# A head's norm behind the second projection instead of the first, and the finest level tiles in one bank of PSUM

## The chip, the core and the metric

The kernel runs on one core of a Trainium2 chip. The metric is the device time of one execution in microseconds (us), as the median of several runs. TensorE does the matrix products, VectorE (DVE) and ScalarE (ACT) read PSUM and work on SBUF, GpSimd (POOL) works on SBUF alone, and the queue of SyncE (SP) starts most transfers. Each engine executes its instructions strictly in the order in which they are written and waits on semaphores.

## What is computed

The reference is one layer of a decoder trunk for a prompt of 1024 tokens and 8 sample sequences. One input projection feeds three parallel token mixers: a gated linear recurrence with 4 heads of 128 keys by 128 values (branch A), a second recurrence behind a convolution (B) and a sparse attention (C). The merged result goes through an output projection and a layer norm. The change touches branch A alone:

```
qa = silu(aq); log_f = logaddexp(log(lb), log1p(-lb) + log_sigmoid(af)); ka = -expm1(log_f)
oa, s_new = hgrn2_chunked(qa, ka, ai, log_f, s0)        # prompt; hgrn2_recurrent for the samples
ya = (group_rms(oa).reshape(B, T, A_WIDTH) * a_norm_g) * silu(az)
```

`group_rms` divides each head's output by the root of its mean square over the 128 values: this is the norm that moves.

## The kernel before

All engines walk through one written plan, `a_items(h)` for h = 0 to 4. In pass h the projections of head h are computed (items P0, P1, ...; in pass 4 gate projections G0, G1, ... take their place) and between them stand the chunks of the recurrence of head h-1 (items R0 to R7, one for each 128 tokens), and the norm of head h-2 (item N). Each engine runs its own part of an item, in the plan's order.

- A projection item is 24 products of 128 by 344 columns (`split_product`, L1023): 8 blocks of the inner dimension, three products each of a high and a low part. P0 to P2 fill two banks in turn (ring `pq`), the others use banks 3 and 4 (ring `pf`). ScalarE takes a tanh or a copy of the result (L1993, L1999), VectorE multiplies (L2550).
- R c is, on TensorE, `a_levels`: the products of chunk c's attention matrix, 7 levels from 64 x 64 down to 32 x 32 blocks (L1566 to L1579), then a transpose (L1586) for the key, and then `a_output` of the chunk before (L1599 to L1602). Levels of 8 down to 1 (i = 3 to 6) each have a tile of 128 columns: three in bank 5, the last in bank 6. On VectorE R c is `a_att`: it waits for the level products, and five COPY_PREDICATED (L2594) gather their tiles under masks. The fifth signals `att_masked`, for which the next chunk's `a_levels` waits, since it writes the same tiles.
- N is, on TensorE, `a_norm`: three products of the squares with a matrix of ones (L1617 into bank 2 behind the key's transpose, and two by L1620 into the ring `pf`). They wait for `sq_ready`, ScalarE's square (L2059) of the head's output at the end of the pass before (item Q). ScalarE then takes Ln of the three results (L2070) and Exp of the whole (L2072), each behind a load of its function table, and signals `rms_ready`. VectorE multiplies the output by gain and gate (L2614) and, after `rms_ready`, by the norm (L2616).

Item N stands in passes 2, 3 and 4 right behind the first projection (heads 0, 1 and 2; below the first, second and third norm). Head 3's norm is the last item of all. The first R0's transpose in a pass waits for `rms_ready`, because the norm's product lies in its bank (L1585).

Of the kernel before, what the change touches and what calls it, by code (L numbers as in the profile page):

```python
# [27 lines left out]
P = 128  # L28
# [5 lines left out]
TC = NS + T  # L34
CH = TC // 3
# [237 lines left out]
def layer_program(nc, ctx, a, o):  # L273
# [13 lines left out]
    ps = ctx.enter_context(nc.psum_tensor("ps", [P, 8, 512], F32))  # L287
# [234 lines left out]
    def e(name):  # L522

        if name not in ev:
            ev[name] = sem(name)
        return ev[name]  # L540
# [38 lines left out]
    def a_items(h):  # L579


        if h == 4:
            plan = "G0 N G1 R0 G2 R1 G3 R2 G4 R3 G5 R4 G6 S R5 G7 R6 G8 O R7 G9 Z Q G10 G11 N"
        elif h % 2:
            plan = "P0 N P1 R0 P2 R1 P3 P4 R2 P5 R3 P6 P7 R4 P8 S R5 P9 R6 P10 O R7 P11 Z F Q"
        else:
            plan = "P0 N P1 R0 P2 R1 P3 P4 R2 P5 R3 P6 R4 P7 S R5 P8 R6 P9 O R7 P10 Z F Q"
        items, norm = [], h - 2
        for x in plan.split():
            if x == "N":  # L590
                if norm >= 0:
                    items.append((x, norm))
                norm += 1
            elif x[0] in "PGF" or h:
                items.append((x[0], int(x[1:] or 0)))
        return items

    def a_product(h, i):

# [412 lines left out]
    def _(pe):  # L1012
        mm = nc.tensor.matmul
# [542 lines left out]
        def a_levels(h, c):  # L1556
            S = AS[h % 2]
            q = 4 * h + c // 2
            pe.wait_ge(e("x_ready"), q + 1)
            pe.wait_ge(e("att_masked"), natt[0] + 1)  # L1560
            natt[0] += 1
            cc = slice(P * (c % 2), P * (c % 2) + P)
            tc = slice(NS + P * c, NS + P * c + P)
            for g in range(4):
                gp, c0 = slice(32 * g, 32 * g + 32), 32 * g
                mm(ps[gp, 5, c0:c0 + 32], lhsT=XQ[:, q % 2, 9, cc.start + c0:cc.start + c0 + 32],  # L1566
                   rhs=S["q"][:, tc.start + c0:tc.start + c0 + 32], start=True, stop=True)
            for i in range(3):
                m = LEVELS[i]
                for s0 in range(0, P, 2 * m):  # L1570
                    c0 = P * (c % 2) + s0
                    mm(ps[s0:s0 + m, 5, s0 + m:s0 + 2 * m], lhsT=XQ[:, q % 2, i, c0:c0 + m], rhs=XQ[:, q % 2, i, c0 + m:c0 + 2 * m],  # L1572
                       start=True, stop=True)
            for i in range(3, 7):
                bank, p0 = (5, P * (i - 2)) if i < 6 else (6, 0)
                for g in range(4):
                    c0 = 32 * g
                    x = XQ[:, q % 2, i, cc.start + c0:cc.start + c0 + 32]
                    last = mm(ps[c0:c0 + 32, bank, p0 + c0:p0 + c0 + 32], lhsT=x, rhs=x, start=True, stop=True)  # L1579
            last.then_inc(e("att_full"), 1)  # L1580
            i = 8 * h + c
            if i >= 1:
                pe.wait_ge(e("kot_ready"), i)
            if c == 0 and h:
                pe.wait_ge(e("rms_ready"), h)  # L1585
            nc.tensor.transpose(ps[:, 2, 0:P], XQ[:, q % 2, 8, cc], ID).then_inc(e("kot_full"), 1)  # L1586

        def a_output(h, c):
# [23 lines left out]
        def a_norm(h):  # L1612
            sq = AS[h % 2]["bk"]
            pe.wait_ge(e("sq_ready"), h + 1)
            if h < 3:
                pe.wait_ge(e("kot_ready"), 8 * h + 8)
                mm(ps[:, 2, P:P + CH], lhsT=ONES, rhs=sq[:, 2 * CH:TC], start=True, stop=True)  # L1617
            for c in range(2 if h < 3 else 3):
                b = pf.acquire(pe)
                mm(ps[:, 3 + b, 0:CH], lhsT=ONES, rhs=sq[:, CH * c:CH * c + CH], start=True, stop=True).then_inc(pf.full, 1)  # L1620
# [122 lines left out]
    def _(act):  # L1743
# [317 lines left out]
        def a_norm(h):  # L2061

            sq = AS[h % 2]["bk"]
            for c in range(3):
                if c < 2 or h == 3:
                    b = pf.take(act)
                    src, free = ps[:, 3 + b, 0:CH], pf.free
                else:
                    src, free = ps[:, 2, P:P + CH], None
                st(A(sq[:, CH * c:CH * c + CH], src, ACT.Ln, bias=G[:, GEPS:GEPS + 1], scale=0.25 / P), free)  # L2070

            st(A(sq, sq, ACT.Exp, scale=-0.5), e("rms_ready"))  # L2072
# [98 lines left out]
    def _(v):  # L2171
# [412 lines left out]
        def a_att(h, c):  # L2584
            natt[0] += 1
            i = 8 * h + c
            if i == 0:
                st(V.memset(ATT, 0.0))
            v.wait_ge(e("att_full"), natt[0])
            if i >= 2:  # L2590
                v.wait_ge(e("chunk_full"), i - 1)
            for l in range(5):
                tile = ps[:, 5, P * l:P * l + P] if l < 4 else ps[:, 6, 0:P]
                st(V.copy_predicated(ATT[:, i % 2], LM[:, 2 + l].bitcast(U16), tile), e("att_masked") if l == 4 else None)  # L2594
            st.mark(e("att_ready"))

# [226 lines left out]
```

## Time and profile before

| | us |
|---|---|
| median of 3 runs | 1654.55 |
| lowest and highest | 1649.14, 1655.98 |
| the profiled execution's own time | 1653.34 |
| its span in the profile | 1651.3 |
| TensorE busy | 1528.5 (93%) |
| TensorE loading weights | 1372.2 (83%) |
| VectorE, ScalarE, GpSimd busy | 828.8, 563.8, 569.1 |
| TensorE's share of the chain that ended last | 53% (42% of the span is L1023) |

The page's busy shares say which engine fills the span; the chain that ended last says what the end waited for at each moment. A row of a timeline gives an operation's start, its busy time and, in brackets, how long the engine had been idle before it and what released it.

### The profile page before, as it was taken

Reading aid. Unit: us, or ns where it says so; the run is one execution under the profiler, and the core shown is the slowest. Engines: PE = TensorE matmul, PEld = TensorE weight load, DVE = VectorE, ACT = ScalarE, POOL = GpSimd, SP = SyncE. Lnnn points to the kernel's source line nnn. Section 1 sums busy time; section 2 is a strip of 40 time slices with the busy share of each in tenths; the row PEclk is TensorE's granted clock in tenths of the full one; section 3 lists DMA queues with packets and bytes.
Section 4 is the critical chain, followed back from the end, with each engine's and each line's share of the span. In section 5 each row is a group of like instructions: output and inputs, shape, how many; then the busy total and the mean of one; then the engine's idle time right before and its main releaser. Section 6 shows DMA issues by size and latency. Waiting matters only on the chain.

```text
span 1651.3 us, 35632 instructions
## 1 busy us (share of the span) xinstructions
PE 1528.5 (93%) x14484; PEld 1372.2 (83%) x14484; DVE 828.8 (50%) x1555; ACT 563.8 (34%) x1128; POOL 569.1 (34%) x833
## 2 busy tenths in 40 slices
PE   5899889999998999999989999999899988999997
PEld 4899866666667888888879998889798887999997
DVE  3640557666661233333324256757552655456588
ACT  1213135545451333333312353745432765001100
POOL 2233000000004111221032577888772252346700
PEclk8999989999998999999999999999899999999999
DMA  9510120000006344434251411203032121544422
GB/s 332 176 51 28 28 91 2 1 1 1 1 20 177 90 117 132 121 117 120 70 182 41 129 27 39 81 27 105 31 102 74 29 60 33 200 154 144 165 91 78
DMA packets 136852, 143.20 MB, mean 87 GB/s; under 512 B 17110, under 2 KB 126706, under 8 KB 135922
## 3 DMA queue, kind: packets, MB, share of 16 engines
q1 hardware_dynamic: 127362, 127.03, 25.0%
q10 hardware_dynamic: 9328, 13.90, 2.3%
q8 instruction: 115, 1.88, 0.5%
q14 instruction: 47, 0.39, 0.1%
HBM read 115.62 MB, written 29.40 MB: 88 GB/s over the span
## 4 chain that ended last, share of the span: by engine, by line
PE 53%; POOL 6%; ACT 4%; DVE 3%; issue 2%; DMA 0%; SPq 0%; ACTq 0%; DVEq 0%; POOLq 0%; PEldq 0%
PE ps L1023 42%; PE ps L1385 2%; PE ps L1372 2%; POOL w_lo L907 1%; ACT xq L2042 1%; POOL vs_spread L977 1%; POOL dd L957 1%; PE ps L1034 1%; POOL dd L958 1%; POOL sts L974 1%; PE ps L1609 1%; POOL w_hi L903 1%; POOL sts L979 1%; PE ps L1572 1%; PE ps L1668 1%
## 5 line engine op out<-in xcount | busy, mean ns | idle before, releaser
L1023 PE MATMUL ps<-w_hi,h_hi 128*128 128x256 f32 x704 | 203.7, 289 | 5.9 <-DVEq L152 2.9
L1023 PE MATMUL ps<-h_hi,w_hi 128*128 128x344 f32 x600 | 199.9, 333 | 9.2 <-POOL w_lo L907 6.1
L1023 PE MATMUL ps<-w_lo,h_hi 128*128 128x256 f32 x704 | 198.9, 283 | 1.1 <-issue 1.1
L1023 PE MATMUL ps<-w_hi,h_lo 128*128 128x256 f32 x704 | 198.8, 282 | 0.0
L1023 PE MATMUL ps<-h_lo,w_hi 128*128 128x344 f32 x600 | 194.1, 324 | 0.0
L1023 PE MATMUL ps<-h_hi,w_lo 128*128 128x344 f32 x600 | 193.6, 323 | 0.0
L903 POOL CAST w_hi<-w_raw 128x512 fp32r<-128x512 f32 (+1 forms) x96 | 64.9, 676 | 280.1 <-DMA w_raw<-in_w_in 107.0
L907 POOL TENSOR_TENSOR w_lo<-w_raw,w_hi 128x256 fp32r<-128x256 f32 (+1 forms) x192 | 151.0, 817 | 3.9
L1023 PE MATMUL ps<-h_hi,wg_hi 128*128 128x344 f32 x432 | 143.8, 333 | 1.4 <-DVE pcs L2420 0.8
L1023 PEld LDWEIGHTS ps<-w_hi,h_hi 128*128 128x128 f32 x704 | 134.2, 191 | 10.0 <-DVEq L152 3.3
L1023 PE MATMUL ps<-h_lo,wg_hi 128*128 128x344 f32 x432 | 138.9, 322 | 0.0
L1023 PE MATMUL ps<-h_hi,wg_lo 128*128 128x344 f32 x432 | 138.8, 321 | 0.0
L1023 PEld LDWEIGHTS ps<-w_lo,h_hi 128*128 128x128 f32 x704 | 134.1, 190 | 0.0
L1023 PEld LDWEIGHTS ps<-w_hi,h_lo 128*128 128x128 f32 x704 | 134.0, 190 | 0.0
L920 POOL TENSOR_TENSOR qt<-qt,to 128x512 f32<-128x512 f32 x16 | 20.3, 1267 | 314.7 <-DVE to L2390 314.7
L1023 PEld LDWEIGHTS ps<-h_hi,w_hi 128*128 128x128 f32 x600 | 115.5, 193 | 12.4 <-POOL w_lo L907 6.8
L1023 PEld LDWEIGHTS ps<-h_lo,w_hi 128*128 128x128 f32 x600 | 115.0, 192 | 0.7 <-issue 0.2
L1023 PEld LDWEIGHTS ps<-h_hi,w_lo 128*128 128x128 f32 x600 | 115.0, 192 | 0.0
L1862 ACT ACTIVATE pr<-ps,nm 128x640 f32<-128x640 f32 (+7 forms) x128 | 88.4, 697 | 39.0 <-DVE nm L2350 32.7
L930 POOL CAST wg_hi<-w_raw 128x512 fp32r<-128x512 f32 x36 | 22.1, 614 | 220.9 <-PE ps L1023 177.9
L1023 PEld LDWEIGHTS ps<-h_hi,wg_hi 128*128 128x128 f32 x432 | 82.1, 190 | 12.3 <-issue 8.3
L1281 PE MATMUL ps<-const_g,pr 128*128 128x128 f32 x560 | 82.0, 279 | 10.2 <-DVE pt L2358 3.5
(463 smaller groups left out, 3568.3 us busy)
## 6 DMA issues: line engine op xcount, KB each, us to landing
w_raw<-in_w_in SPq DMA_DIRECT2D x46, 512.0 KB, 4.4
sgm<-gate_spill SPq DMA_DIRECT2D x22, 516.0 KB, 6.2
gate_spill<-gate_stage ACTq DMA_DIRECT2D x54, 172.0 KB, 2.4
w_raw<-in_w_in SPq DMA_DIRECT2D x34, 256.0 KB, 4.6
adw<-in_ada_w SPq DMA_DIRECT2D x8, 1024.0 KB, 11.6
pgc<-in_cache_nsa_kv SPq DMA_DIRECT2D x64, 128.0 KB, 2.8
pg<-in_cache_nsa_kv SPq DMA_DIRECT2D x64, 128.0 KB
w_raw<-in_w_branch SPq DMA_DIRECT2D x12, 512.0 KB, 5.0
```

The lines of the kernel that those rows point to most:

```text
L903: last = nc.gpsimd.tensor_copy(hi[:, kj, 0:width], raw[:, j:j + 2])
L907: last = nc.gpsimd.tensor_tensor(lo[:, kj, 0:width], raw[:, j:j + 1], hi[:, kj, 0:width].bitcast(F32), SUB)
L920: st(nc.gpsimd.tensor_tensor(d3, d3, TO[:, i % 2, :].rearrange("p (a c) -> p a c", a=4), ADD), e("to_added"))
L930: st(nc.gpsimd.tensor_copy(hi[:, j:j + 4], raw[:, j:j + 4]))
L957: st(nc.gpsimd.tensor_tensor(dv[:, :, 0, :], ref, kv_[:, :, 0, :], SUB))
L958: st.fire(nc.gpsimd.tensor_tensor(dv[:, :, 1, :], bv[:, :, 1, :], ref, SUB), e("d_ready"))
L974: st(nc.gpsimd.tensor_tensor(STS[:, b:b + 2], STS[:, b:b + 2], decay[:, b:b + 2].unsqueeze(2).to_broadcast([P, 2, P]), MUL))
L1023: last = mm(out, lhsT=l, rhs=r, start=(first and i == 0 and j == 0), stop=(final and i == n - 1 and j == 2), skip_group_check=joint)
L1281: last = nc.tensor.transpose(ps[:, 4 + way, P * i:P * i + P], PR[:, u % 2, P * j:P * j + P], ID)
L1372: last = mm(ps[half, bank + q, P * j:P * j + P], lhsT=buf[:, s, j, 256 * par + c:256 * par + c + 64], rhs=ID, start=True, stop=True)
L1385: last = mm(ps[:, 3, P * c:P * c + P], lhsT=W1S[:, c, j].rearrange("p x o -> p (x o)"), rhs=CMT[:, c, :, j, :], start=(j == 0), stop=(j == 7))
L1862: st.fire(A(PR[:, u % 2, P * n * g:P * n * g + P * n], src, ACT.Exp, bias=NM[:, 4 * (u % 2) + g:4 * (u % 2) + g + 1], scale=-1.0, accum_ou ...
```

## The change

The norm item N moves behind the second projection in every plan (`P0 P1 N R0` for `P0 N P1 R0`). The four finest level tiles now begin 32 columns apart in bank 5, so that they overlap in columns but not in the 32 x 32 blocks that are used. Bank 6 is thereby free and takes the norm's first product. With it go two waits of TensorE: the norm's for the last key of the head before (`kot_ready`) and the transpose's for `rms_ready`. One is added: the norm's first product waits for the `rms_ready` of the norm before.

```diff
--- before.py
+++ after.py
@@ -580,11 +580,11 @@
 
 
         if h == 4:
-            plan = "G0 N G1 R0 G2 R1 G3 R2 G4 R3 G5 R4 G6 S R5 G7 R6 G8 O R7 G9 Z Q G10 G11 N"
+            plan = "G0 G1 N R0 G2 R1 G3 R2 G4 R3 G5 R4 G6 S R5 G7 R6 G8 O R7 G9 Z Q G10 G11 N"
         elif h % 2:
-            plan = "P0 N P1 R0 P2 R1 P3 P4 R2 P5 R3 P6 P7 R4 P8 S R5 P9 R6 P10 O R7 P11 Z F Q"
+            plan = "P0 P1 N R0 P2 R1 P3 P4 R2 P5 R3 P6 P7 R4 P8 S R5 P9 R6 P10 O R7 P11 Z F Q"
         else:
-            plan = "P0 N P1 R0 P2 R1 P3 P4 R2 P5 R3 P6 R4 P7 S R5 P8 R6 P9 O R7 P10 Z F Q"
+            plan = "P0 P1 N R0 P2 R1 P3 P4 R2 P5 R3 P6 R4 P7 S R5 P8 R6 P9 O R7 P10 Z F Q"
         items, norm = [], h - 2
         for x in plan.split():
             if x == "N":
@@ -594,6 +594,10 @@
             elif x[0] in "PGF" or h:
                 items.append((x[0], int(x[1:] or 0)))
         return items
+
+    def level_tile(l):
+
+        return P + 32 * (l - 1) if l else 0
 
     def a_product(h, i):
 
@@ -1572,17 +1576,15 @@
                     mm(ps[s0:s0 + m, 5, s0 + m:s0 + 2 * m], lhsT=XQ[:, q % 2, i, c0:c0 + m], rhs=XQ[:, q % 2, i, c0 + m:c0 + 2 * m],
                        start=True, stop=True)
             for i in range(3, 7):
-                bank, p0 = (5, P * (i - 2)) if i < 6 else (6, 0)
+                p0 = level_tile(i - 2)
                 for g in range(4):
                     c0 = 32 * g
                     x = XQ[:, q % 2, i, cc.start + c0:cc.start + c0 + 32]
-                    last = mm(ps[c0:c0 + 32, bank, p0 + c0:p0 + c0 + 32], lhsT=x, rhs=x, start=True, stop=True)
+                    last = mm(ps[c0:c0 + 32, 5, p0 + c0:p0 + c0 + 32], lhsT=x, rhs=x, start=True, stop=True)
             last.then_inc(e("att_full"), 1)
             i = 8 * h + c
             if i >= 1:
                 pe.wait_ge(e("kot_ready"), i)
-            if c == 0 and h:
-                pe.wait_ge(e("rms_ready"), h)
             nc.tensor.transpose(ps[:, 2, 0:P], XQ[:, q % 2, 8, cc], ID).then_inc(e("kot_full"), 1)
 
         def a_output(h, c):
@@ -1613,8 +1615,9 @@
             sq = AS[h % 2]["bk"]
             pe.wait_ge(e("sq_ready"), h + 1)
             if h < 3:
-                pe.wait_ge(e("kot_ready"), 8 * h + 8)
-                mm(ps[:, 2, P:P + CH], lhsT=ONES, rhs=sq[:, 2 * CH:TC], start=True, stop=True)
+                if h:
+                    pe.wait_ge(e("rms_ready"), h)
+                mm(ps[:, 6, 0:CH], lhsT=ONES, rhs=sq[:, 2 * CH:TC], start=True, stop=True)
             for c in range(2 if h < 3 else 3):
                 b = pf.acquire(pe)
                 mm(ps[:, 3 + b, 0:CH], lhsT=ONES, rhs=sq[:, CH * c:CH * c + CH], start=True, stop=True).then_inc(pf.full, 1)
@@ -2066,7 +2069,7 @@
                     b = pf.take(act)
                     src, free = ps[:, 3 + b, 0:CH], pf.free
                 else:
-                    src, free = ps[:, 2, P:P + CH], None
+                    src, free = ps[:, 6, 0:CH], None
                 st(A(sq[:, CH * c:CH * c + CH], src, ACT.Ln, bias=G[:, GEPS:GEPS + 1], scale=0.25 / P), free)
 
             st(A(sq, sq, ACT.Exp, scale=-0.5), e("rms_ready"))
@@ -2590,7 +2593,7 @@
             if i >= 2:
                 v.wait_ge(e("chunk_full"), i - 1)
             for l in range(5):
-                tile = ps[:, 5, P * l:P * l + P] if l < 4 else ps[:, 6, 0:P]
+                tile = ps[:, 5, level_tile(l):level_tile(l) + P]
                 st(V.copy_predicated(ATT[:, i % 2], LM[:, 2 + l].bitcast(U16), tile), e("att_masked") if l == 4 else None)
             st.mark(e("att_ready"))
```

On TensorE, pass 2 around the first norm, before (`ak` holds the squares, `aq` and `xq` the recurrence's factors; the names behind "waits" are semaphores):

```order
L1023 MATMUL ps<-h_hi,w_lo 128x344
L1617 MATMUL ps<-ak_168,ones 128x344 [waits kot_ready,sq_ready]
L1620 MATMUL ps<-ak_168,ones 128x344 [waits pf_free] x2
L1023 MATMUL ps<-h_hi,w_hi 128x344 [waits pq_free]
...
L1566 MATMUL ps<-aq_171,xq 32x32 [waits x_ready,att_masked,pf_free,pq_free]
...
L1586 MATMUL ps<-const_g,xq 128x128 [waits rms_ready,kot_ready]
L1023 MATMUL ps<-h_hi,w_hi 128x344 [waits pq_free]
...
L1566 MATMUL ps<-aq_171,xq 32x32 [waits att_masked,x_ready]
```

And with the change:

```order
L1027 MATMUL ps<-h_hi,w_lo 128x344
L1620 MATMUL ps<-ak_168,ones 128x344 [waits sq_ready]
L1623 MATMUL ps<-ak_168,ones 128x344 [waits pf_free] x2
L1570 MATMUL ps<-aq_171,xq 32x32 [waits x_ready,att_masked,pf_free,pq_free]
...
L1588 MATMUL ps<-const_g,xq 128x128 [waits kot_ready]
L1027 MATMUL ps<-h_hi,w_hi 128x344 [waits pq_free]
...
L1570 MATMUL ps<-aq_171,xq 32x32 [waits att_masked,x_ready]
```

The 24 products of P1, which stood between the norm and the levels of R0, now stand ahead of the norm; P2, between the levels of R0 and those of R1, stays where it was.

On VectorE at the same place, before (`sga` is ScalarE's tanh, `ot` the head's output, `att` the attention matrix, `lm` the masks):

```order
L2571 TENSOR_TENSOR xq<-xq,aq_171 128x256 [waits eb_ready,own_dve]
L2550 SCALAR_TENSOR_TENSOR aq_167<-sga,ps 128x344 [waits own_dve,d_exp,sg_ready]
L2614 SCALAR_TENSOR_TENSOR ot<-ot,prm,az_170 128x1032 [waits sq_ready,pq_free]
L2616 TENSOR_TENSOR ot<-ot,ak_168 128x1032 [waits rms_ready,own_dve]
L2550 SCALAR_TENSOR_TENSOR aq_167<-sga,ps 128x344 [waits sg_ready,ya_done]
L2594 COPY_PREDICATED att<-lm,ps 128x128 [waits chunk_full,att_full,pq_free]
L2594 COPY_PREDICATED att<-lm,ps 128x128 [waits own_dve] x4
```

And with the change:

```order
L2574 TENSOR_TENSOR xq<-xq,aq_171 128x256 [waits eb_ready,own_dve]
L2553 SCALAR_TENSOR_TENSOR aq_167<-sga,ps 128x344 [waits own_dve,d_exp,sg_ready]
L2553 SCALAR_TENSOR_TENSOR aq_167<-sga,ps 128x344 [waits sg_ready,pq_free]
L2617 SCALAR_TENSOR_TENSOR ot<-ot,prm,az_170 128x1032 [waits sq_ready,pq_free]
L2619 TENSOR_TENSOR ot<-ot,ak_168 128x1032 [waits rms_ready,own_dve]
L2597 COPY_PREDICATED att<-lm,ps 128x128 [waits chunk_full,att_full,ya_done]
L2597 COPY_PREDICATED att<-lm,ps 128x128 [waits own_dve] x4
```

P1's multiplication has moved ahead of the norm's two operations; the masks of R0 stand directly behind them.

## Rows read from the trace of the kernel before

**Rows 1.** The page: the span, and TensorE's granted clock in 40 slices, in tenths.
```profile
span 1651.3 us, 35632 instructions
...
PEclk8999989999998999999999999999899999999999
```

**Rows 2.** Timeline of TensorE, first norm: start, us busy, operation, idle before and releaser.
```profile
1032.62 0.32 PE L1023 MATMUL ps<-h_hi,w_lo 128*128 128x344 f32 x1
...
1034.38 0.85 PE L1617 MATMUL ps<-ak,ones 128*128 128x344 f32 x2 [1.44 <-ACT ak L2059]
...
1035.96 0.58 PE L1023 MATMUL ps<-h_hi,w_hi 128*128 128x344 f32 x1
...
1040.08 0.27 PE L1566 MATMUL ps<-aq,xq 128*32 128x32 f32 x8
...
1041.41 0.30 PE L1586 MATMUL ps<-const_g,xq 128*128 128x128 f32 x1 [0.27 <-ACT ak L2072]
...
1045.40 0.27 PE L1566 MATMUL ps<-aq,xq 128*32 128x32 f32 x8
```

**Rows 3.** The chain that ended last, 1020 to 1060 us: one projection group of 24 products.
```profile
1041.71 3.77 PE ps L1023 x24
```

**Rows 4.** Timeline of ScalarE, first norm.
```profile
1035.88 1.28 ACT L2070 ACT_TABLE_LOAD   x1 [1.07 <-PE ps L1620]
...
1038.90 1.28 ACT L2072 ACT_TABLE_LOAD   x1
...
1040.20 1.06 ACT L2072 ACTIVATE ak<-ak 128x1032 f32<-128x1032 f32 x1
```

**Rows 5.** Timeline of VectorE, first norm.
```profile
1041.36 1.32 DVE L2616 TENSOR_TENSOR ot<-ot,ak 128x1032 f32<-128x1032 f32 x1 [3.22 <-ACT ak L2072]
...
1043.26 1.67 DVE L2594 COPY_PREDICATED att<-lm,ps 128x128 f32<-128x128 uint16 x5
```

**Rows 6.** Timeline of TensorE, second and third norm.
```profile
1105.70 0.56 PE L1617 MATMUL ps<-ak,ones 128*128 128x344 f32 x1 [1.79 <-ACT ak L2059]
...
1116.72 0.27 PE L1566 MATMUL ps<-aq,xq 128*32 128x32 f32 x8
...
1180.79 0.84 PE L1617 MATMUL ps<-ak,ones 128*128 128x344 f32 x2 [1.44 <-ACT ak L2059]
...
1184.19 0.43 PE L1023 MATMUL ps<-h_hi,w_hi 128*128 128x344 f32 x1 [1.40 <-ACT ak L2070]
...
1193.19 0.27 PE L1566 MATMUL ps<-aq,xq 128*32 128x32 f32 x8
```

**Rows 7.** Timeline of VectorE, second and third norm.
```profile
1112.69 1.33 DVE L2616 TENSOR_TENSOR ot<-ot,ak 128x1032 f32<-128x1032 f32 x1 [4.07 <-ACT ak L2072]
...
1187.78 1.45 DVE L2616 TENSOR_TENSOR ot<-ot,ak 128x1032 f32<-128x1032 f32 x1 [3.86 <-ACT ak L2072]
```

**Rows 8.** Waits of GpSimd, 1116 to 1163 us: for whom, total, times, longest.
```profile
POOL dd L957 <- ACT xq L2042: 2.9, 2, 2.3
POOL w_hi L903 <- PEq L1540: 0.8, 1, 0.8
```

**Rows 9.** Timeline of TensorE: three longer waits elsewhere.
```profile
1017.39 2.56 PE L1609 MATMUL ps<-aq,sts 128*128 128x1 f32 x16 [1.95 <-POOL sts L979]
...
1162.51 3.57 PE L1609 MATMUL ps<-aq,sts 128*128 128x1 f32 x16 [2.65 <-POOL sts L979]
...
1331.50 0.65 PE L1023 MATMUL ps<-h_hi,w_hi 128*128 128x344 f32 x1 [4.41 <-POOL w_lo L907]
```

**Rows 10.** Windows of 1 us: length, PE busy (instructions), granted clock, DMA, GB/s.
```profile
1161.00:1162.00 1.00, 0.00 (x0) 0.95 0.00 0
1162.00:1163.00 1.00, 0.49 (x3) 0.50 0.00 0
...
1172.00:1173.00 1.00, 1.00 (x8) 0.93 0.00 0
...
1335.00:1336.00 1.00, 1.00 (x6) 0.51 0.00 0
```

## The prediction

> **What bounds the kernel now.** I read the page first: TensorE is busy nearly throughout, at its full clock (2.4 GHz) in most slices and below it in a few [rows 1]. Then I listed TensorE's waits in the stretch of branch A, and read the timelines of the engines at each moved norm. TensorE bounds this stretch, so a microsecond in which it has nothing to do counts, unless a later wait gives it back.
>
> At the first norm the last product of P0 starts at 1032.62; the norm's first product comes at 1034.38 after 1.44 us idle, for ScalarE's square. So P0 ends at 1032.94. P1 follows the norm at 1035.96, the levels of R0 come at 1040.08, the transpose at 1041.41 after 0.27 us idle for the norm's Exp, P2 then, and the levels of R1 at 1045.40 [rows 2]. P2 takes 3.77 us [rows 3]. The norm itself occupies TensorE for 1.58 us (1034.38 to 1035.96).
>
> ScalarE is slower at the norm: a table load of 1.28 us from 1035.88, three Ln, a second load, and an Exp that ends at 1040.20 + 1.06 = 1041.26 [rows 4]. VectorE, which had been idle for 3.22 us for this, multiplies from 1041.36 for 1.32 us and masks R0's tiles from 1043.26 for 1.67 us, to 1044.93 [rows 5]. The levels of R1 wait for these masks. Before the change they are ready 0.47 us ahead of TensorE. That margin is what the reader should keep in view.
>
> At the second norm TensorE idles 1.79 us, at the third 1.44 and then 1.40 us, since G1 needs a bank of ring `pf` that the norm's second product holds until ScalarE has read it [rows 6].
>
> **The change part by part.** Removed: the idle time ahead of the norms, 1.44 + 1.79 + 1.44 us; the third norm's 1.40 us for a bank; and 0.27 us twice at the transpose (seen at the first norm; the second's is taken as the same). Together 6.6 us. P1 fills the time instead, and the square is ready when it ends.
>
> Added: P1 no longer stands between the norm and the masks of R0. Call T0 the start of the norm's products. From T0 to VectorE's multiplication is 6.98 us (1034.38 to 1041.36) [rows 2, 5], and 6.99 us at both others (1105.70 to 1112.69, 1180.79 to 1187.78) [rows 6, 7]. This chain goes through the products, two table loads and the Exp, and nothing of it gets shorter. Behind it VectorE has 1.32, 1.33 or 1.45 us of multiplication and 1.67 us of masks, with some 0.03 us between, and some 0.1 us until TensorE is released (my estimate, after the 0.10 us from the Exp's end at 1041.26 to 1041.36). So R1 can start at T0 + 10.1, 10.1 and 10.2 us. TensorE itself gets there sooner: norm 1.58, levels 1.33 - 0.27 = 1.06, transpose about 0.3, P2 3.77, in all T0 + 6.7 us. A new wait of 3.4 us ahead of R1's levels takes the place of the old ones.
>
> T0 in the new order is the end of P0 plus one projection group:
>
> - first norm: 1032.94 + 3.77 = 1036.71; R1 at 1046.8 where it was 1045.40 [rows 2, 3, 5]: 1.4 us later.
> - second: 1105.70 - 1.79 + 3.77 = 1107.68; R1 at 1117.8 where it was 1116.72 [rows 6, 7]: 1.1 us later.
> - third: 1180.79 - 1.44 + 3.77 = 1183.12; R1 at 1193.35 where it was 1193.19 [rows 6, 7]: 0.2 us later. G2 needs the bank as G1 did, 3.40 us behind the norm's start (1180.79 to 1184.19); by then 2.9 us of other work have passed, so the wait splits into some 0.4 and 3.1 us.
>
> The sum of these is 2.7 us longer.
>
> Then the clock. In the windows, TensorE idle from 1159.86 to 1162.51 lost its full clock near 1161.95; the granted clock was 0.50 (1.2 GHz) until about 1172 [rows 9, 10]. I went through all of TensorE's waits of 1.3 us and more behind the start-up: six are of 2.65 to 4.41 us (the shortest and longest are shown), and at each the clock fell; three are of about 2 us (1.95 is shown), and at two of them it fell; none of the shorter ones, the norms' 1.44 and 1.79 us among them, made it fall [rows 2, 6, 9]. The change has three waits of 3.1 to 3.4 us where it had 1.4 to 1.8 us. A fall costs half of the low time in which TensorE works: 1162.51 to 1172.07 is 9.6 us, so 4.8 us; behind the wait that ended at 1331.50 the clock was back near 1335.9, so 2.2 us [rows 9, 10]. Behind R1's levels dense projections follow at once, so I take 3.0 us, between the bounds: 9.0 us for three falls, with 6.6 and 14.4 us as bounds, and 0 if none falls.
>
> The Trainium skill, "TensorE: Matmul & The Clock Gate", section "Why this matters for your kernels", advises to leave no long idle gaps between bursts of products, because the engine then goes back to half rate. By that rule the sum is the one with falls; without it, it is the 2.7 us alone. The trace agrees with it at all six waits of 2.65 us and more.
>
> What costs nothing: the overlapping tiles take the same 16 products per chunk and the same five mask reads, so neither TensorE nor VectorE has more to do. The added wait on the previous `rms_ready` is over by tens of microseconds (1041.26 against 1105.70). ScalarE's two table loads stay two. Its key copy and the nine Exp of the next pair of chunks start some 2 us later, and with them GpSimd's last differences; what needs them is R2, two projection groups (7.5 us) behind R1, so they stay hidden by some microsecond. If that cover were gone, R2 would be late by another 1 us.
>
> Does a later wait give the delay back? TensorE waits 2.65 us for GpSimd's sample states at 1162.51 [rows 9]. But GpSimd had waited 0.8 us for TensorE to release weights, and had 2.9 us of waits for ScalarE's Exp, in the 1116 to 1163 us that lead there [rows 8]; the former is at 1131.9, and behind it GpSimd works with hardly a gap. So GpSimd starts that work later by as much as TensorE is late, and the wait stays.
>
> Sum: 1653.34 + 2.7 + 9.0 = 1665.0 us against the profiled execution. The median of the runs is 1654.55, 1.2 us above it, within their spread of 1649.14 to 1655.98; I give 1665.
>
> **The rivals.** What a measurement of this kernel can tell from no change is about 0.5%, 8.3 us.
>
> - The new waits come, but the clock mostly holds (none or one fall). For it speaks that a fall at a 2 us wait is not certain; against it, that six of six longer ones fell. It gives +2.7 to +5.7 us, 1657 to 1660. Chance 0.18.
> - Not slower, the gain stays: this happens if the masks of R0 end before TensorE is through with P2. Then 6.6 us are saved, 1648 us. It needs the norm's chain of 6.98 us plus 3.0 us on VectorE to shrink to under 6.7 us; break-even is where it shrinks by 0.9 us at each norm. Nothing in the change shortens it, except that weights of ones may load ahead while P1 still runs (0.2 us at most). With a fall of the clock saved near 1162 as well (4.8 us) it would be past 0.5%. Chance 0.06.
> - The change does nothing: the delay is taken back in the waits of 1.95 to 2.65 us for the sample states, as far as GpSimd isn't held up by TensorE, and falls of the clock only change places. 1654 us. Chance 0.08.
>
> **How the numbers follow.** My forecast, new waits with two or three falls, has 0.68: 1653.34 + 2.7 + 2 x 2.2 = 1660.4 at least and + 2.7 + 14.4 = 1670.4 at most. The range of 1656 to 1671 takes in nearly all of the first rival as well, and leaves out the other two. Slower by over 0.5% (above 1662.8): nearly all of the forecast's 0.68, less the 0.04 in which two falls are cheap, plus 0.01 from a first rival with a dear fall: 0.65. Faster by over 0.5%: half of the second rival, 0.03. Within 0.5%: 0.32.
>
> **What would show it.** Right: TensorE's norm products directly behind P1, with no idle time; a wait of 3.1 to 3.4 us ahead of the levels of R1 (L1570) in passes 2, 3 and 4, released by VectorE; a granted clock of 0.50 behind at least two of them; TensorE's idle time at the norm gone. VectorE's masks of R0 directly behind its norm multiplication. Wrong would be: masks of R0 ready before P2 ends; a clock at 1.00 through all three waits; or a wait for the sample states that has shrunk by what the norms lost.

## The result: slower by a third of a per cent

Measured together, the changed kernel takes 1656.66 us (median, 1652.62 to 1662.35) and the kernel before 1652.36 us: a ratio of 1.0033 with a 95% interval of 1.0024 to 1.0043 (the quotient of the two medians alone is 1.0026). Two more measurements of the unedited change gave 1.0049 and 1.0038 (runs 5 and 10 below). By the means, each against the kernel before measured beside it, the change is 5.0, 8.8 and 7.1 us slower, with standard errors of 0.8 to 1.0 us. All its 30 executions have a mean of 1658.3 us, and 72 of the kernel before, those of runs 1 to 12, have one of 1653.0 us. That is 5.3 us (standard error 0.6), but it mixes chips in unequal parts. The forecast was 10.4 us above the median shown and 11.7 us above the profiled execution. The direction and the waits came as forecast; the price of the clock did not.

The page of the changed kernel, its profiled execution (1658.82 us):

```profile
span 1656.9 us, 35628 instructions
...
PEclk7999999999998999999999999999999999999999
```

The span is 5.6 us longer than before's [rows 1]. The tenths of the granted clock look no worse, so falls can't be counted there: each lasts under 11 us, a quarter of a slice of 41 us.

TensorE's timeline at the three norms, the rows that answer to [rows 2, 6]:

```profile
1036.17 0.74 PE L1620 MATMUL ps<-ak,ones 128*128 128x344 f32 x2
...
1037.99 0.27 PE L1570 MATMUL ps<-aq,xq 128*32 128x32 f32 x8
...
1042.76 0.32 PE L1027 MATMUL ps<-h_hi,w_lo 128*128 128x344 f32 x1
1046.11 0.34 PE L1570 MATMUL ps<-aq,xq 128*32 128x32 f32 x8 [3.04 <-DVE att L2597]
...
1057.91 0.27 PE L1570 MATMUL ps<-aq,xq 128*32 128x32 f32 x8
...
1110.82 0.74 PE L1620 MATMUL ps<-ak,ones 128*128 128x344 f32 x2
...
1120.77 0.34 PE L1570 MATMUL ps<-aq,xq 128*32 128x32 f32 x8 [3.05 <-DVE att L2597]
...
1131.23 0.27 PE L1570 MATMUL ps<-aq,xq 128*32 128x32 f32 x8
...
1186.93 0.74 PE L1620 MATMUL ps<-ak,ones 128*128 128x344 f32 x2
...
1196.87 0.27 PE L1570 MATMUL ps<-aq,xq 128*32 128x32 f32 x8 [2.61 <-DVE att L2597]
...
1203.53 0.27 PE L1570 MATMUL ps<-aq,xq 128*32 128x32 f32 x8 [1.12 <-DVEq L152]
```

What matters in them is that the norm's products (L1620) have no idle time ahead of them any more, and that the levels of R1 (the second L1570 of a norm) now wait 3.04, 3.05 and 2.61 us for VectorE's masks. The last row is the third norm's R2, which waits as well. VectorE there, against [rows 5]:

```profile
1037.54 1.29 DVE L2617 SCALAR_TENSOR_TENSOR ot<-ot,prm,az 128x1032 f32<-128x1032 f32 x1
1043.06 1.23 DVE L2619 TENSOR_TENSOR ot<-ot,ak 128x1032 f32<-128x1032 f32 x1 [4.23 <-ACT ak L2075]
1044.33 1.64 DVE L2597 COPY_PREDICATED att<-lm,ps 128x128 f32<-128x128 uint16 x5
```

The level products of R0 had ended by 1039.1, but their masks start at 1044.33, behind a multiplication for which VectorE idles 4.23 us. From the norm's first product to R1 it is 1046.11 - 1036.17 = 9.94 us; the forecast was 10.1.

Windows around R1 of the first norm (four rows), of the second (three) and of the third (the columns are length, then busy us and instructions of PE, PEld, DVE, ACT, POOL, then the granted clock, DMA share and GB/s):

```profile
1044.00:1045.00 1.00, 0.00 (x0) 0.00 (x0) 0.90 (x3) 0.94 (x3) 0.92 (x2) 1.00 0.00 0
1045.00:1046.00 1.00, 0.00 (x0) 0.00 (x0) 0.90 (x3) 0.91 (x4) 1.00 (x3) 0.68 0.92 326
1050.00:1051.00 1.00, 1.00 (x6) 1.00 (x5) 0.90 (x4) 0.00 (x0) 1.00 (x2) 0.50 0.01 2
1053.00:1054.00 1.00, 1.00 (x8) 1.00 (x7) 0.92 (x2) 0.00 (x0) 0.92 (x3) 1.00 1.13 342
1120.00:1121.00 1.00, 0.23 (x8) 0.23 (x8) 0.82 (x3) 0.94 (x3) 1.00 (x3) 0.72 0.98 343
1123.00:1124.00 1.00, 1.00 (x6) 1.00 (x6) 0.96 (x2) 0.40 (x2) 1.00 (x3) 0.57 0.41 115
1124.00:1125.00 1.00, 1.00 (x9) 1.00 (x8) 0.90 (x4) 0.00 (x0) 1.00 (x2) 1.00 0.00 0
1197.00:1203.00 6.00, 5.41 (x83) 4.97 (x78) 5.34 (x15) 3.75 (x10) 5.61 (x13) 1.00 0.57 171
```

The clock fell at the first two waits, for 6.8 and 3.4 us, and held at the third (1.00 from 1197 to 1203). In the profiles of both kernels each stretch of low clock between 1000 and 1260 us lasted 3.4, 6.8 or 10.2 us.

**Where the time went.** One measure serves for all kernels here: the start of a chunk's levels, counted from the end of ScalarE's square (before 1034.32, 1105.64 and 1180.73; after 1033.96, 1108.95 and 1184.72). Up to the square nothing at the norm differs.

| us behind the square's end | norm 1: R1, R2 | norm 2: R1, R2 | norm 3: R1, R2 |
|---|---|---|---|
| before | 11.08, 20.33 | 11.08, 20.33 | 12.46, 17.93 |
| after | 12.15, 23.95 | 11.82, 22.28 | 12.15, 18.81 |
| later | 1.07, 3.62 | 0.74, 1.95 | -0.31, 0.88 |

R1's delay is the late start. What R2 has beyond it at the first two norms is the low clock: 2.5 and 1.2 us. At the third norm the clock held, R1 was 0.3 us early, and R2 0.9 us late by its own wait. From the last levels of pass 1 (before 1020.68) to those of pass 4 (1229.99) the stretch is 5.1 us longer. It is less than the sum of the row, 3.62 + 1.95 + 0.88, because the low clock behind the wait for the sample states, 10.2 us long before [rows 10], was 6.8 us long after. Another execution of the kernel before (run 9) also has 6.8 us there, so this is no work of the change. In the profiles of runs 5 and 10 the stretch is 8.0 and 7.8 us longer than before's.

### The profile page after: what moved, and what is told of

Read it like the earlier page. It is cut to its first block, busy times and chain, and to the rows that moved or that the text cites. A ratio compares the mean times of both kernels' runs of the same rounds, so it can differ in the third digit from the quotient of the medians.

```text
span 1656.9 us, 35628 instructions
## 1 busy us (share of the span) xinstructions
PE 1531.5 (92%) x14484; PEld 1374.8 (83%) x14484; DVE 828.1 (50%) x1555; ACT 564.3 (34%) x1128; POOL 571.3 (34%) x833
## 4 chain that ended last, share of the span: by engine, by line
PE 55%; POOL 6%; DVE 4%; ACT 3%; issue 2%; DMA 0%; SPq 0%; ACTq 0%; DVEq 0%; POOLq 0%; PEldq 0%
PE ps L1027 43%; PE ps L1389 2%; PE ps L1376 2%; POOL w_lo L911 1%; POOL vs_spread L981 1%; POOL dd L961 1%; PE ps L1038 1%; POOL dd L962 1%; POOL w_hi L907 1%; POOL sts L978 1%; PE ps L1611 1%; PE ps L1671 1%; POOL sts L983 1%; PE ps L1576 0%; DVE att L2597 0%
## 5 line engine op out<-in xcount | busy, mean ns | idle before, releaser
L1027 PEld LDWEIGHTS ps<-h_hi,w_hi 128*128 128x128 f32 x600 | 115.8, 193 | 10.2 <-POOL w_lo L911 6.5
L1865 ACT ACTIVATE pr<-ps,nm 128x640 f32<-128x640 f32 (+7 forms) x128 | 88.5, 697 | 38.0 <-DVE nm L2353 31.6
```

Of the source, the lines that this page charges most:

```text
L1027: last = mm(out, lhsT=l, rhs=r, start=(first and i == 0 and j == 0), stop=(final and i == n - 1 and j == 2), skip_group_check=joint)
L1865: st.fire(A(PR[:, u % 2, P * n * g:P * n * g + P * n], src, ACT.Exp, bias=NM[:, 4 * (u % 2) + g:4 * (u % 2) + g + 1], scale=-1.0, accum_ou ...
```

## The experiments

The twelve runs in the order in which they ran. Each ratio is against the kernel before on the same chip, with its 95% interval; runs 5 to 8 ran on one chip, the others on another.

| run | median us (executions) | ratio |
|---|---|---|
| 1 products in the wait | 1658.37 (8) | 1.0028 (1.0016 to 1.0040) |
| 2 masks ahead of the norm on VectorE | 1650.37 (8) | 0.9977 (0.9967 to 0.9988) |
| 3 tiles and bank alone | 1650.80 (12) | 0.9984 (0.9975 to 0.9992) |
| 4 order alone | 1663.68 (5) | 1.0064 (1.0051 to 1.0077) |
| 5 the change again | 1659.93 (5) | 1.0049 (1.0035 to 1.0063) |
| 6 products in all four waits | 1657.57 (5) | 1.0036 (1.0022 to 1.0050) |
| 7 no table loads | 1651.45 (11) | 0.9997 (0.9988 to 1.0006) |
| 8 masks and tanh first | 1657.88 (5) | 1.0045 (1.0030 to 1.0059) |
| 9 the kernel before again | 1654.21 (12) | 1.0000 (0.9989 to 1.0011) |
| 10 the change, third time | 1660.08 (6) | 1.0038 (1.0024 to 1.0052) |
| 11 third norm alone | 1655.21 (12) | 1.0006 (0.9995 to 1.0017) |
| 12 masks first at two norms | 1649.40 (6) | 0.9970 (0.9958 to 0.9982) |

The theory was that the wait ahead of R1 is paid twice, by late starts and by the clock; the rivals were that the clock costs little, and that the tiles' new places cost something of their own.

### 1 and 6: is it the clock?

The idle time ahead of R1 is filled with products whose result nobody reads, into a free bank, so that TensorE keeps busy and R1 starts no sooner.

```diff
+        def keep_busy(h, n):
+            pe.wait_ge(pf.free, pf.p - 1)
+            b = (pf.p - pf.p0) % 2
+            w = wslot(U_A + 2 * h if h < 4 else U_G)
+            for k in range(n):
+                mm(ps[:, 3 + b, 0:CH], lhsT=w[0][:, k % 8, 0:P], rhs=H[0][:, k % 8, 0:CH], start=True, stop=True)
...
+                    if h >= 2 and i == 1:
+                        keep_busy(h, 16)
                     a_levels(h - 1, i)
```

Run 1:

> The changed kernel, with 16 products of 344 columns into a free bank behind P2 (G2), ahead of the levels of R1, in passes 2, 3 and 4: some 2.5 us of work without use, inside a wait that the changed kernel's profile shows as 3.04, 3.05 and 2.61 us. Theory one, two terms: the changed kernel lost 2.7 us by late starts of R1 and R2 and about 3 us by the clock that fell at these waits. Then this kernel keeps the 2.7 us and loses the rest: ratio to the kernel before 1.0010 to 1.0020, idle time ahead of R1 under 0.7 us, granted clock 1.00 there. Theory two, no clock term: the falls only change places, all 5.5 us are late starts. Then the ratio stays at 1.0033.

Run 6 has 17 such products in passes 2 and 3, 15 in pass 4, and 8 more ahead of pass 4's R2:

> As the first kernel with useless products, now 17 of them ahead of R1 in passes 2 and 3, 15 in pass 4, and 8 ahead of R2 in pass 4, where that kernel had a wait of 1.56 us and a fall. Idle time left ahead of R1 some 0.4 us. Theory one, a clock term on top of late starts: the late starts remain (R2 1.1 and 0.8 us later than before, counted from the end of the square, at the first two norms, R3 0.9 us at the third), no fall between the norm and R3: ratio 1.0012 to 1.0022, 0.001 to 0.002 below the changed kernel beside it. Theory two, no clock term on balance: the same ratio as the changed kernel beside it.

TensorE's timeline of run 6, R1 and R2 of the second norm, and a window over both:

```profile
1120.58 0.27 PE L1570 MATMUL ps<-aq,xq 128*32 128x32 f32 x8 [0.37 <-DVE att L2609]
...
1129.83 0.27 PE L1570 MATMUL ps<-aq,xq 128*32 128x32 f32 x8
```

```profile
1116.00:1126.00 10.00, 9.63 (x111) 9.23 (x110) 7.84 (x17) 6.79 (x16) 7.89 (x15) 1.00 0.42 130
```

The idle time was 0.25 to 0.37 us, no fall was left between the norms and R3, and R1 and R2 came 12.18 and 21.43 us behind the square's end at the first norm, 11.88 and 21.13 at the second, 12.17 and 18.91 at the third. Against before that is 1.1, 0.8 and 1.0 us later at R2: the late starts without the clock, 2.9 us in all. The clock's extra 2.5 and 1.2 us of the changed kernel are gone. So at the place the clock's share is shown. Run 1 is alike at R1 (idle time of 0.39 to 0.52 us, clock at 1.00), but kept a wait of 1.56 us ahead of pass 4's R2, with a fall behind it.

In the time of the whole kernel the share is hard to find, and both ratios lie above what a theory with a clock term expected. Run 6 is 2.7 us (mean) faster than run 5 on the same chip. Run 1, by its distance from the kernel before beside it, is 2.8 us faster than run 10 and 0.7 us faster than the first measurement; each of these three has a standard error of 1.0 to 1.3 us. Pooled, runs 1 and 6 have a mean of 1657.6 us in 13 executions, 0.8 us (standard error 0.7) below the change's 30.

An execution's mean granted clock gives its low time, the time at half clock: twice the span times the part of the full clock that is missing. Further below it serves to compare whole executions.

### 2: is it the order on VectorE?

```diff
                     a_att(h - 1, i)
+                    if i == 0 and h >= 2:
+                        a_norm(h - 2)
...
-                elif kind == "N":
+                elif kind == "N" and i == 3:
                     a_norm(i)
```

> The changed kernel, but on VectorE the norm's two operations of heads 0, 1 and 2 stand behind the masks of R0 and ahead of the factors. Theory one, the masks of R0 behind the norm's chain make R1 late: then the wait of 2.6 to 3.0 us ahead of R1 goes, the levels of R1 start some 6.8 us behind the norm's products instead of 9.94. R2 then waits up to 1.1 us for the factors, which come at the same time as before. Net 1 to 1.5 us per norm faster than the kernel before at the first two, about 0 at the third, and no falls there: ratio to before 0.996 to 0.999. Theory two, the wait has another cause (ScalarE's key copy, or the bank): the wait and the ratio of 1.0033 stay.

VectorE and TensorE at the first norm:

```profile
1038.31 1.66 DVE L2597 COPY_PREDICATED att<-lm,ps 128x128 f32<-128x128 uint16 x5 [1.66 <-PE ps L1583]
...
1042.20 1.23 DVE L2619 TENSOR_TENSOR ot<-ot,ak 128x1032 f32<-128x1032 f32 x1 [0.79 <-ACT ak L2075]
1043.47 2.96 DVE L2580 TENSOR_TENSOR xq<-xq,aq 128x128 f32<-128x128 f32 x5
```

```profile
1042.15 0.27 PE L1570 MATMUL ps<-aq,xq 128*32 128x32 f32 x8
1052.40 0.27 PE L1570 MATMUL ps<-aq,xq 128*32 128x32 f32 x8 [0.93 <-DVEq L152]
```

The masks start 5.2 us behind the square's end, where the changed kernel has them at 10.4, R1 waits for nothing, and the kernel is faster than both others. The wait did not vanish whole: VectorE's factors for chunks 2 and 3 (L2580) are late by the norm, and R2 waits 0.93, 0.94 and, in pass 4, 2.36 us for them. R2 still comes 1.0, 1.4 and 0.6 us earlier than before; a fall behind the last of these waits makes pass 4's R3 0.8 us late.

### 3 and 4: the two halves of the change

Run 3 has the changed kernel's tiles, bank and waits with before's three plans; run 4 has before's tiles, bank and waits with the new plans.

> One part of the change alone: the overlapping tiles and the norm's product in bank 6, with the norm behind the first projection as in the kernel before. Theory one, all of the loss comes from the moved norm: ratio 0.999 to 1.000, since only the 0.27 us twice at the transpose go. Rival, products or mask reads in one crowded bank are slower: five mask reads longer than 1.67 us or the level products longer, 32 chunks long, ratio 1.002 to 1.003.

> The other part alone: the norm behind the second projection, with the tiles, the norm's product and the two waits as in the kernel before. The transpose of R0 waits for the norm's Exp, which is ready 6.9 us behind the norm's start, when the levels end 2.7 us behind it. Theory one: a wait of some 4.2 us ahead of P2 (G2), R1 at the norm's start + 11.0 us, so 1 us per norm later than in the changed kernel, 5.7 us later than before in all, and falls of the clock at most of the waits, 3 to 8 us more: ratio 1.005 to 1.008. Theory without a clock term: 5.7 + 2.8 us for what the changed kernel shows beyond 2.7, whatever its cause, ratio 1.005.

Run 3, R0's transpose and R1 of the first norm, and run 4, R0's transpose, in TensorE's timeline:

```profile
1040.85 0.33 PE L1588 MATMUL ps<-const_g,xq 128*128 128x128 f32 x1
1044.87 0.27 PE L1570 MATMUL ps<-aq,xq 128*32 128x32 f32 x8
```

```profile
1041.95 0.45 PE L1586 MATMUL ps<-const_g,xq 128*128 128x128 f32 x1 [4.03 <-ACT ak L2072]
```

The freed bank takes the transpose's 0.27 us away at the first two norms; levels and masks last as long as before. That is a gain of 0.6 us by the timeline; the measured 0.16% (2.6 us) has an interval down to 1.3 us, and is more than was expected. Its low time is 85.7 us against 91.1 beside it, which fits the rest but doesn't show its cause. So the overlapping tiles cost nothing that these runs show, and what slows the change is the order. In before's bank the order costs more: the transpose waits 4.03 us for the Exp at all three norms, ahead of P2 instead of behind it, and R1 comes 15.78, 14.33 and 15.28 us behind the square's end, the low clock behind each of these waits included.

### 7: how much of it are the table loads?

ScalarE takes Abs in place of Ln for the norms of heads 0 to 2, which needs no other function table than the Exp. This kernel computes other values for these norms.

```diff
-ACT.Ln, bias=G[:, GEPS:GEPS + 1]
+ACT.Ln if h == 3 else ACT.Abs, bias=G[:, GEPS:GEPS + 1]
```

> The changed kernel, in which ScalarE takes an absolute value in place of the Ln for heads 0, 1 and 2, so that no function table is loaded at these norms (the norm's values are then not the reference's). The chain from the norm's products to the masks' end is 2.56 us shorter. Theory one, this chain sets R1: the wait ahead of R1 shrinks from 3.0 to some 0.5 us, R1 starts 9.6 us behind the square's end where it was 12.15 (11.08 before), R2 too comes earlier than before: ratio 0.997 to 0.999. Rival, VectorE's or GpSimd's other work sets R1: the wait stays above 2 us.

ScalarE's and TensorE's timelines, first norm:

```profile
1034.71 1.71 ACT L2073 ACTIVATE ak<-ps,const_g 128x344 f32<-128x344 f32 x3 [0.70 <-PE ps L1623]
1036.45 1.07 ACT L2075 ACTIVATE ak<-ak 128x1032 f32<-128x1032 f32 x1
```

```profile
1040.70 0.27 PE L1570 MATMUL ps<-aq,xq 128*32 128x32 f32 x8 [0.50 <-DVE att L2597]
```

Two loads of 1.28 us gone take 2.5 us off the wait at the first two norms (3.04 to 0.50, 3.05 to 0.57) and 1.9 us at the third (2.61 to 0.75). R1 comes 9.64, 9.34 and 9.89 us behind the square's end, earlier than before. So the loads are most of the wait. The ratio is 0.0036 to 0.0052 below the change's, but misses the expected 0.997 to 0.999: R2 comes 1.4, 1.7 and 0.7 us earlier than before, and the mean is lower by only 0.9 us (standard error 0.8). In pass 4 R2 waits 1.79 us with a fall behind it, and low time is 92.9 us against 85.1 beside it. What brought the other low time wasn't looked into.

### 8: a further step that failed

On top of run 2, ScalarE takes the tanh of the third projection group ahead of R0's Exp, and VectorE all factors of chunks 2 and 3 in R1.

```diff
+                    if i == 0 and h >= 2:
+                        a_group(h, 2) if h < 4 else a_gate(2)
...
+                    if h >= 2 and i < 2:
+                        if i:
+                            a_factors(h - 1, 1, range(8))
```

> The kernel with VectorE's norm behind the masks of R0, and in passes 2, 3 and 4 also: ScalarE's tanh of P2 (G2) ahead of the nine Exp of R0, and VectorE's factors of the second pair of chunks all in R1, behind its masks. In its parent R2 waited 0.93 us twice for these factors. Theory one: that wait goes, R2 starts 18.3 us behind the square's end where it was 20.33 before: 2.0 and 2.4 us saved at the first two norms, little at the third, where GpSimd's differences come late: ratio 0.996 to 0.998. If the masks of R1 or the factors are late in the new order: a new wait ahead of R2, ratio as its parent's 0.9977 or above.

TensorE's timeline, R2 of the first and the third norm:

```profile
1051.47 0.27 PE L1570 MATMUL ps<-aq,xq 128*32 128x32 f32 x8 [1.94 <-DVEq L152]
...
1201.40 0.33 PE L1570 MATMUL ps<-aq,xq 128*32 128x32 f32 x8 [6.17 <-DVEq L152]
```

VectorE's, first norm, R1:

```profile
1047.12 0.29 DVE L2609 COPY ot<-ps 128x128 f32<-128x128 f32 x1 [3.38 <-SPq L781]
```

R2 waits longer instead of less, 6.17 us in pass 4, where only one group lies between R1 and R2. VectorE's factors are what R2 needs. They were put off until R1, and there they stand behind two copies for which VectorE idles 3.38 us (4.25 us at the third norm). What the tanh alone does wasn't tried.

### 5, 9 and 10: the same kernels again

> The changed kernel once more, unedited, for a second look at which waits the clock falls at and for a time beside the next kernel on one chip. Both theories: ratio 1.0025 to 1.0040, the wait of some 3 us ahead of R1 three times. The theory of a clock term: a fall at two or three of these waits; the theory that falls only change places: one or two, and fewer falls than in the kernel before elsewhere between 1000 and 1250 us.

> The kernel before, unedited, to see what its own falls of the clock do from one execution to the next. Theory (falls away from the norms change place by themselves; the 1.4 and 1.8 us waits at the norms cause none): ratio 1.000 within 0.0015, span 1649 to 1655 us, no fall of the granted clock at the norms (1034, 1106, 1181 us), falls at the 2 us and longer waits that are not all those of the first profile, and the stretch from the last levels of pass 1 to the last levels of pass 4 within 1.5 us of 209.3. Rival (the falls belong to the program): the same list of falls to within one, and the stretch within 0.3 us of 209.3.

> The changed kernel, unedited, a third profile. Theory (2.75 us of late starts always, and a clock term that varies with the execution, 0 to 3 us a wait): waits ahead of R1 of 3.0, 3.0, 2.6 to 2.9 us, falls at two or three of them, the stretch from the last levels of pass 1 to the last of pass 4 longer than before's by 3 to 9 us, ratio 1.003 to 1.005. Rival (the forecast's 9.0 us for the clock): falls at all three, the stretch longer by 10 to 12 us, ratio 1.006 or more.

The change's waits were the same each time at the first two norms, as these rows of run 10 show beside those of the first profile, and so were the offsets of R1 (12.18 and 11.82) and of R2 (24.03 and 22.33): falls at both in all three profiles, at 2.5 to 2.6 and 1.2 to 1.3 us each time. The third norm varies:

```profile
1045.59 0.34 PE L1570 MATMUL ps<-aq,xq 128*32 128x32 f32 x8 [3.04 <-DVE att L2597]
...
1120.25 0.34 PE L1570 MATMUL ps<-aq,xq 128*32 128x32 f32 x8 [3.05 <-DVE att L2597]
...
1196.69 0.27 PE L1570 MATMUL ps<-aq,xq 128*32 128x32 f32 x8 [2.89 <-DVE att L2597]
...
1203.79 0.27 PE L1570 MATMUL ps<-aq,xq 128*32 128x32 f32 x8 [1.55 <-DVEq L152]
1211.04 0.27 PE L1570 MATMUL ps<-aq,xq 128*32 128x32 f32 x8
```

There R1's wait of 2.89 us left the clock alone, and behind R2's 1.55 us came a fall of 3.4 us: R2 to R3 took 7.25 us where it takes 5.68, 1.6 us more. R2 itself came 1.6 us later than before, counted from the square, where it was 0.9 us in the first profile: VectorE's operations ahead of it took longer, the norm's last multiplication 1.50 us for 1.23 and the five factors behind the masks 2.88 us for 2.65. Run 5 is alike, and its ratio lies above the 1.0025 to 1.0040 that were expected.

The kernel before, in run 9, had a stretch from pass 1 to pass 4 only 0.6 us shorter than the first time, but with other falls in it. The wait for the sample states was the same (2.64 us for 2.65), the low clock behind it was not. The same 10 us in both, before and run 9:

```profile
1162.00:1172.00 10.00, 9.49 (x88) 9.23 (x89) 2.31 (x8) 0.28 (x1) 5.36 (x13) 0.50 0.01 2
```

```profile
1089.00:1090.00 1.00, 1.00 (x9) 1.00 (x8) 0.81 (x3) 0.28 (x1) 1.00 (x2) 0.69 0.00 0
1090.00:1091.00 1.00, 1.00 (x6) 1.00 (x6) 0.79 (x4) 0.00 (x0) 0.92 (x3) 0.50 0.00 0
...
1161.00:1171.00 10.00, 10.00 (x100) 9.74 (x100) 2.31 (x8) 0.28 (x1) 4.73 (x12) 0.66 0.01 2
```

It was back at full clock at 1168, 6.8 us behind, and this gave 1.3 us back in that stretch. On the other hand a fall of 3.4 us stands at 1089.5, where TensorE's longest wait in the 9 us ahead was 0.38 us and the first profile shows none, and it costs 1.5 us. The profiles of runs 1 to 4, 6 and 8 have one near the same chunk (R7 of pass 2) too, the three of the change have none there. So an execution's falls are partly the program's and partly its own.

### 11 and 12: norm by norm, and the best version

Run 11 has the new plan in pass 4 alone. Run 12 has run 2's order in passes 2 and 3, and before's plan in pass 4. Its edit against run 2:

```diff
-            plan = "G0 G1 N R0 G2 R1 ..."
+            plan = "G0 N G1 R0 G2 R1 ..."
...
-                    if i == 0 and h >= 2:
+                    if i == 0 and h in (2, 3):
                         a_norm(h - 2)
...
-                elif kind == "N" and i == 3:
+                elif kind == "N" and h == 4:
                     a_norm(i)
```

> The changed kernel with before's order in passes 2 and 3, so that only the third norm stands behind the second projection; the tiles share their bank. Theory (late starts are R1's 1.1 and 0.8 us at the first two norms, less 0.3 each from the bank, and at the third 0.9 us at R2, since the factors of chunks 2 and 3 are late): no wait ahead of R1 in passes 2 and 3, 2.6 to 3.0 us in pass 4 and 1.0 to 1.6 us ahead of R2; pass 4's R2 0.9 us later behind the end of the square than before; in all -0.3 - 0.3 + 0.9 = +0.3 us and 0 to 3 us of clock, ratio 1.000 to 1.002. Rival (the forecast's terms: 0.2 us and a fall of 3.0 us at this norm, nothing at R2): ratio 1.002 or more, with R2 no later than R1.

> The order P1 N in passes 2 and 3 with VectorE's norm behind the masks of R0, and before's order in pass 4; the tiles share their bank. Theory (at the third norm the new order costs R2 and R3 0.8 us even with the masks first, before's order with the free bank costs nothing there): waits of 0.9 us ahead of R2 in passes 2 and 3 only, R2 1.0 us earlier than before at the first two norms, pass 4 as before, ratio 0.997 to 0.999, 0 to 1 us below the kernel with all three norms behind the masks (0.9977). Rival (what made that kernel fast is less low clock, not earlier starts): ratio within 0.0008 of 0.9984, the kernel with the bank alone.

Run 11 answers to the theory in its time (1.0006) and in the stretch from pass 1 to pass 4, 0.06 us longer than before. R1 of pass 4 waited 2.91 us and had a fall, and so R2 had no wait of its own, where I had expected one of 1.0 to 1.6 us. It came 1.65 us later than before, not 0.9.

Run 12, waits of TensorE from 1020 to 1245 us (total, times, longest):

```profile
PE ps L1570 <- DVEq L152: 3.8, 4, 1.1
PE ps L1611 <- POOL sts L983: 3.0, 2, 2.7
PE ps L1620 <- ACT ak L2062: 1.4, 1, 1.4
PE ps L1027 <- ACT ak L2073: 1.4, 1, 1.4
```

R2 comes 19.31 and 18.96 us behind the square's end, 1.0 and 1.4 us earlier than before. Three norms' waits are down to 0.94 us twice and the old 1.4 twice in pass 4. With 0.9970 it is the fastest kernel of the case, though its interval overlaps those of runs 2 and 3. The rival, less low clock and not earlier starts, isn't out: low time is 84.0 us against 88.5 beside it (run 2: 83.6 against 91.1), and the earlier starts give 2.4 of the 4.2 us by which the mean is lower.

## Why the forecast was right and where it was not

**The waits removed** are gone, as forecast, at the norm and the transpose; ahead of G2 TensorE idles 0.14 us (0.4 forecast).

**The wait added** was forecast at 3.4, 3.4 and 3.1 us and measured 3.04, 3.05 and 2.61; R1 came 9.94 us behind the norm's start for 10.1. Runs 2 and 7 show the cause twice: with VectorE's order turned round the wait is gone, with the table loads gone it shrinks by their time.

**The late starts** were forecast at 1.4 + 1.1 + 0.2 = 2.7 us. Counted from the square they are 1.1 + 0.7 + 0.9 = 2.7 us, and run 6 shows them alone as 2.9 us; in runs 5 and 10 the third is 1.6 us, which makes 3.5. The sum is right, one part of it by chance: at the third norm R1 is 0.3 us early, and R2 is 0.9 us late. The step "they stay hidden by some microsecond" failed there: in pass 4 only G3, one group, lies between R1 and R2, not two, and R2 waited 1.12 us for VectorE's factors. The forecast had named its price (1 us) but counted the groups of passes 2 and 3 alone.

**The clock** is the step that failed: "9.0 us for three falls". There were two falls in the profiled execution, of 2.5 and 1.2 us, 3.7 us in all. In two further profiles the third norm had one at R2, of some 1.6 us more. Three things can be read from rows. At low clock one product follows the other at 0.286 us where it was 0.157, so low time costs 45% and not half. Both bounds came from falls with 4.4 and 9.6 us of low clock in which TensorE worked, while two of the six falls that the forecast counted lasted only 3.4 us, as did the second norm's here: those behind the waits of 3.66 and 2.88 us that ended at 1365.86 and 1395.46. At 45% that is 1.5 us, and 1.2 us were measured. In windows of the kernel before, as [rows 10]:

```profile
1366.00:1367.00 1.00, 1.00 (x4) 0.85 0.00 0
...
1370.00:1371.00 1.00, 1.00 (x8) 0.94 0.00 0
1371.00:1372.00 1.00, 1.00 (x8) 1.00 0.00 0
```

And "six of six" waits of 2.65 us and more did not make it certain: at R1 it fell in two of three, and the 2.89 us of runs 5 and 10 left it alone.

Whole executions agree in part. Low time is 94.3 us in the change's 30 executions and 88.9 in the 72 of before, 5.4 us more (standard error 1.8), where three falls of 6 us each would have been 18. In runs 5 and 10 alone it is 14.4 and 12.1 us more than in the kernel before beside them, as the 6.8 + 3.4 + 3.4 us of the falls at their norms would have it. Across the executions of one kernel, a microsecond of low time goes with 0.23 (before) to 0.29 us (after) of time, wherever in the kernel it falls. By that the clock makes 1.2 to 1.6 us of the change, and 2.8 to 4.2 us in runs 5 and 10.

By the timelines late starts and clock are 2.7 + 3.7 = 6.4 us in the first profile and 3.5 + 5.4 = 8.9 us in runs 5 and 10. Less the 1.3 us that the shorter low clock behind the sample states gave back, these are 5.1 and 7.6 us, and the stretches are 5.1, 8.0 and 7.8 us longer. The means are 5.0, 8.8 and 7.1 us higher.

**The rivals.** "The clock mostly holds", +2.7 to +5.7 us, takes in the first measurement's 5.0 us and not the 8.8 and 7.1 of the others, and its mechanism is not what came: the clock did fall, and cheaply. "Not slower" was shown to need a shorter chain on VectorE: runs 2 and 12 get it by order. "Does nothing" is out, by the interval.

**Still open.** Runs 1 and 6 have about before's low time (87.9 us) and late starts of 2.9 us (run 6), but are 4.6 us slower than before, with a standard error of 0.6 (4.4 and 6.1 us against the kernel before beside each). Some 1.7 us of it has no place in their timelines that I could show; whether the useless products cost it or the changed start of what follows wasn't tried. And what decides whether a given wait brings a fall, and how long it lasts, isn't settled by these runs.

## What to carry to other kernels

When an item moves past another on one engine, look at what the same item does on the others: here TensorE's gain was lost because VectorE's part of the norm, with its 7 us chain through ScalarE, moved ahead of masks for which TensorE waits. Let each engine have its own order of the items, urgent and short reads of PSUM ahead of a wait that nothing depends on soon; and count the cover behind a moved item in each pass, since one may have less. Price low clock by the lengths of all its falls, from several executions, and not by the longest; and compare the total low time with that of a kernel before measured beside it.

## What the runs showed of the hardware

- One and the same wait of TensorE, 2.65 and 2.64 us for the sample states, had 10.2 us of low clock behind it in one execution of a kernel and 6.8 us in another. A fall of 3.4 us stood in one at a place with no wait above 0.38 us in the 9 us ahead (1089.5) and was missing in the other.
- Waits of 2.61 and 2.89 us left the clock at 1.00 in the changed kernel, while one of 1.55 us behind the latter had 0.50 behind it. The length of the wait alone doesn't decide. The Trainium skill, "TensorE: Matmul & The Clock Gate", section "Why this matters for your kernels", advises against idle gaps between bursts; runs 2 and 12, which shorten them and have less low time, agree, but these waits show no sharp bound.
- At a granted clock of 0.50 a product of 128 by 344 columns follows the other 0.286 us behind (1.8 times 0.157), as in the changed kernel from 1049 to 1052 us.
- Two function table loads of 1.28 us on ScalarE were worth 2.5 us of TensorE's wait at two norms and 1.9 us at the third (run 7).
